# Layer 1 attention: a head's two score blocks merged into one ahead of the softmax, and the turned block masked twice out of PSUM

## What is computed

```python
nb = s // WINDOW                                  # 8 blocks of 128 tokens
kk = jnp.concatenate([prev(kb), kb], axis=2)      # keys of the block before and of the own block
vv = jnp.concatenate([prev(vb), vb], axis=2)
scores = jnp.einsum('bnqhgd,bnkhd->bnhgqk', qb, kk) * (SWA_HEAD_DIM ** -0.5)
valid = ((rel >= 0) & (rel < WINDOW))[None] & ...
scores = jnp.where(valid[None, :, None, None], scores, -jnp.inf)
m = jnp.maximum(jnp.max(scores, axis=-1), sink)
p = jnp.exp(scores - m[..., None])
denom = jnp.sum(p, axis=-1) + jnp.exp(sink - m)
o = jnp.einsum('bnhgqk,bnkhd->bnhgqd', p, vv) / denom[..., None]
```

## Time and profile before

| what | value |
|---|---|
| median of 3 runs | 2116.43 us (2115.18 to 2119.19) |
| the profiled execution | span 2115.3 us, 1.1 under the median and 0.1 over the fastest run |
| PE busy | 2045.7 us, 97% |
| DVE busy | 1604.8 us, 76% |
| ACT busy | 1361.3 us, 64% |
| POOL busy | 277.7 us, 13% |
| the attention of layer 1 | about 1224 to 1461 us of the span |

### The profile page before, as it was taken

How to read it: one execution, slowest core, us unless ns; L and a number is a source line. 1 busy time by engine, 2 the same in 40 slices (tenths; PEclk the granted TensorE clock), 3 DMA queues, 4 the chain that set the end, 5 groups by cost and what they waited for, 6 DMA issues and landing times. The chain is left out here.

```text
span 2115.3 us, 30221 instructions
## 1 busy us (share of the span) xinstructions
PE 2045.7 (97%) x10536; PEld 1661.4 (79%) x10536; DVE 1604.8 (76%) x2000; ACT 1361.3 (64%) x1794; POOL 277.7 (13%) x334
## 2 busy tenths in 40 slices
PE   8999998998999999999999989999899999999998
PEld 6888876787788888888877856777688888888885
DVE  4551246777888888888886267887898888888886
ACT  5333426653788887878772266675577778888774
POOL 2000000001111121111203320110111111122210
PEclk9999999999999999999999999999999999999999
DMA  4112222215999999999983020011699999999996
GB/s 139 40 60 90 78 72 78 81 65 205 343 381 390 389 389 385 380 378 380 385 317 132 1 90 11 21 61 61 231 383 380 381 384 384 387 388 385 384 363 254
DMA packets 123491, 513.28 MB, mean 243 GB/s; under 512 B 27373, under 2 KB 28490, under 8 KB 89610
## 3 DMA queue, kind: packets, MB, share of 16 engines
q1 hardware_dynamic: 103674, 474.11, 59.7%
q0 software_dynamic: 18576, 33.86, 4.2%
q10 hardware_dynamic: 1152, 4.19, 0.5%
HBM read 495.05 MB, written 50.86 MB: 258 GB/s over the span
## 5 line engine op out<-in xcount | busy, mean ns | idle before, releaser
L542 DVE TENSOR_TENSOR exp_w_lo<-ring_raw,first_w_hi 128x2048 fp32r<-128x2048 f32 x192 | 438.9, 2288 | 33.2 <-ACT first_w_hi L469 33.1
L542 DVE TENSOR_TENSOR exp_w_lo<-ring_raw,exp_w_hi 128x2048 fp32r<-128x2048 f32 x192 | 438.8, 2287 | 27.8 <-ACT exp_w_hi L469 27.8
L469 ACT ACTIVATE exp_w_hi<-ring_raw 128x2048 fp32r<-128x2048 f32 x192 | 367.7, 1918 | 62.1 <-PE exp_up_out L394 27.9
L469 ACT ACTIVATE first_w_hi<-ring_raw 128x2048 fp32r<-128x2048 f32 x188 | 360.7, 1919 | 62.2 <-PE exp_up_out L394 23.6
L339 POOL DMA_INDIRECT y_rows<-exp_y,base_rows_y x63 | 79.8, 1266 | 936.1 <-ACT exp_y L489 936.1
L394 PE MATMUL exp_gate_out<-exp_w_lo,exp_x_hi 128*128 128x512 f32 x512 | 201.1, 393 | 0.0
L394 PE MATMUL exp_y_out<-exp_w_lo,exp_hid_hi 128*128 128x512 f32 x512 | 200.4, 391 | 0.0
L394 PE MATMUL exp_up_out<-exp_w_lo,exp_x_hi 128*128 128x512 f32 x512 | 199.3, 389 | 0.0
L546 DVE TENSOR_TENSOR exp_x_lo<-exp_x_turned,exp_x_hi 128x1024 fp32r<-128x1024 f32 x62 | 75.9, 1224 | 51.4 <-ACT exp_x_hi L473 51.4
L394 PE MATMUL exp_gate_out<-first_w_hi,exp_x_hi 128*128 128x512 f32 x272 | 109.7, 403 | 3.1 <-issue 2.0
L350 POOL DMA_INDIRECT first_x_rows<-u_rows,base_rows_u x64 | 104.9, 1639 | 58.6 <-issue 52.2
(11 more groups left out here) (529 smaller groups left out, 4671.8 us busy)
## 6 DMA issues: line engine op xcount, KB each, us to landing
ring_raw<-in_expert_w_gate_dram SPq DMA_DIRECT2D x128, 1024.0 KB, 11.1
ring_raw<-in_expert_w_up_dram SPq DMA_DIRECT2D x128, 1024.0 KB, 11.6
ring_raw<-in_expert_w_down_dram SPq DMA_DIRECT2D x128, 1024.0 KB, 11.4
l0w_raw<-in_ab_w_in_dram SPq DMA_DIRECT2D x48, 256.0 KB, 2.8
finish_y<-y_rows SPq DMA_DIRECT2D x8, 1024.0 KB, 12.4
ring_raw<-in_swa_w_qkv_dram SPq DMA_DIRECT2D x5, 1024.0 KB, 10.1
ring_raw<-y_rows SPq DMA_DIRECT2D x10, 512.0 KB, 4.9
base_h<-in_x_dram ACTq DMA_DIRECT2D x8, 512.0 KB, 7.0
```

Of the source, the lines that this page charges most:

```text
L469: nc.scalar.activation(split[split_slot(unit)][0][:], raw[raw_slot(unit)][:], ACT.Copy).then_inc(hi_ready, 1)
L542: nc.vector.tensor_tensor(lo[:], raw[raw_slot(unit)][:], hi[:].bitcast(F32), ALU.subtract).then_inc(lo_ready[split_slot(unit)], 1)
```

## The change

The two blocks of a head are merged before the softmax: one 128x128 block holds the own block's score where k <= q and that of the block before where k > q. For G >= 4 `copy_own` (new, ACT) copies the own block's 512 columns out of PSUM into `masked`, and `mask` overwrites the places k > q with the block before by `copy_predicated` under `tri_strict` (DVE, out of PSUM); for G < 4 `mask` adds the large negative number there. The scale moves into the exponential and into the negative top. Maximum, exponentials, sums and scalings then run over 128 columns a head, and `turn` has four transposes, into one bank of `turned`, alternately the first and the second. Instead of ACT's copies, DVE's `band_probs` (new) multiplies the turned block out of PSUM by each of two complementary masks (`band`) into the two halves of `prob_t`: the block before first, then the own one. `weigh` is as it was. On DVE the order becomes `band_probs(G)`, `denominators(G+1)`, `mask(G+2)`, `out_low(G)`; on ACT `copy_own(G+2)` and `norm_even(G+1)` come ahead of `out_high(G)`. The table `units` becomes two units at each of its eight places.

```diff
@@ -833,7 +833,7 @@
...
-        ("swa_add", [P, 2, P], F32),
+        ("band", [P, 2, P], F32),
...
@@ -868,7 +868,7 @@
...
-                        ("causal_add", 0.0), ("last_row", 0.0), ("swa_add", 0.0), ("lr_up", 0.0)):
+                        ("causal_add", 0.0), ("last_row", 0.0), ("band", 1.0), ("lr_up", 0.0)):
...
@@ -882,9 +882,9 @@
...
-    for slot, (pattern, step), op in ((0, up, ALU.is_gt), (1, down, ALU.is_ge)):
-        part = c["swa_add"][:, slot]
-        nc.gpsimd.affine_select(out=part, in_=part, pattern=pattern, compare_op=op, fill=NEG,
+    for slot, (pattern, step), op in ((0, down, ALU.is_gt), (1, up, ALU.is_ge)):
+        part = c["band"][:, slot]
+        nc.gpsimd.affine_select(out=part, in_=part, pattern=pattern, compare_op=op, fill=0.0,
...
@@ -2291,11 +2291,13 @@
...
+        by_head = lambda x: x.rearrange("p (h n) -> p h n", h=PER)
...
-        masked = [work[n][:] for n in (3, 4, 5)]
+        masked = [work[n][:, 0:BANK] for n in (3, 4, 5)]
+        turned_at = lambda G: turned[:, PER * (G % 2):PER * (G % 2 + 1)]
...
@@ -2602,20 +2604,15 @@
...
-                n = G // GROUPS
...
-                p_of = heads4(masked[G % 3])
-                for b in range(0 if n else 1, 2):
-                    if b == 0 and G > GROUPS:
-                        pe.wait_ge(s["early_copied"], G - GROUPS)
-                    if b == 1 and G > 0:
-                        pe.wait_ge(s["prob_copied"], G)
-                    for i in range(PER):
-                        last = nc.tensor.transpose(turned[:, PER * b + i], p_of[:, i, b], c["ident"][:])
-                    last.then_inc(s["prob_turned" if b else "early_turned"], 1)
+                if G > 1:
+                    pe.wait_ge(s["own_made"], G - 1)
+                for i in range(PER):
+                    last = nc.tensor.transpose(turned_at(G)[:, i], by_head(masked[G % 3])[:, i], c["ident"][:])
+                last.then_inc(s["prob_turned"], 1)
...
@@ -2627,9 +2624,9 @@
...
-                        pe.wait_ge(s["early_copied"], G - GROUPS + 1)
+                        pe.wait_ge(s["prev_made"], G - GROUPS + 1)
...
-                        pe.wait_ge(s["prob_copied"], G + 1)
+                        pe.wait_ge(s["own_made"], G + 1)
...
@@ -2706,7 +2703,7 @@
...
-            units = {(0, 0): (0, 3), (0, 1): (3, 4), (1, 0): (4, 7), (1, 1): (7, 8), (2, 0): (8, 9), (2, 1): (9, 10), (3, 0): (10, 14), (3, 1): (14, 16)}
+            units = {(0, 0): (0, 2), (0, 1): (2, 4), (1, 0): (4, 6), (1, 1): (6, 8), (2, 0): (8, 10), (2, 1): (10, 12), (3, 0): (12, 14), (3, 1): (14, 16)}
...
@@ -2822,31 +2819,25 @@
                 a.activation(w_hi[:, k], w_raw[:, k], ACT.Copy).then_inc(s["w_hi_made"], 1)
 
             def exponents(G):
-                j, first = G % 3, 0 if G >= GROUPS else P
+                j = G % 3
                 act.wait_ge(s["tops_made"], G + 1)
                 for i in range(PER):
-                    span = slice(i * 2 * P + first, (i + 1) * 2 * P)
-                    a.activation(masked[j][:, span], masked[j][:, span], ACT.Exp, bias=neg_top[j][:, i:i + 1], accum_out=total[j][:, i:i + 1])
+                    own = by_head(masked[j])[:, i]
+                    a.activation(own, own, ACT.Exp, bias=neg_top[j][:, i:i + 1], scale=HEAD_DIM ** -0.5, accum_out=total[j][:, i:i + 1])
                 a.activation(sink_part[j][:], sink_part[j][:], ACT.Exp).then_inc(s["prob_made"], 1)
 
             def norm_even(G):
-                j, first = G % 3, 0 if G >= GROUPS else P
+                j = G % 3
                 act.wait_ge(s["inv_made"], G + 1)
                 for i in range(2):
-                    span = slice(i * 2 * P + first, (i + 1) * 2 * P)
-                    last = a.activation(masked[j][:, span], masked[j][:, span], ACT.Copy, scale=inv[j][:, i:i + 1])
+                    own = by_head(masked[j])[:, i]
+                    last = a.activation(own, own, ACT.Copy, scale=inv[j][:, i:i + 1])
                 last.then_inc(s["even_normed"], 1)
 
-            def copy_turned(G):
-                if G >= 1:
-                    act.wait_ge(s["out_ready"], G)
-                for b in range(0 if G >= GROUPS else 1, 2):
-                    if b == 0:
-                        act.wait_ge(s["early_turned"], G - GROUPS + 1)
-                    else:
-                        act.wait_ge(s["prob_turned"], G + 1)
-                    part = slice(PER * b, PER * (b + 1))
-                    a.activation(prob_t.rearrange("p (k q) -> p k q", q=P)[:, part], turned[:, part], ACT.Copy).then_inc(s["prob_copied" if b else "early_copied"], 1)
+            def copy_own(G):
+                act.wait_ge(s["scored"], G + 1)
+                act.wait_ge(s["prob_turned"], G - 2)
+                a.activation(by_head(masked[G % 3]), heads4(scores)[:, :, 1], ACT.Copy).then_inc(s["own_copied"], 1)
 
             def out_high(G):
                 n, g = G // GROUPS, G % GROUPS
...
@@ -2904,11 +2895,13 @@
             exponents(1)
             for G in range(LAST):
                 g, w = G % GROUPS, G // GROUPS - 2
+                if 1 < G < LAST - 2:
+                    copy_own(G + 2)
                 if w >= 0 and g < 2:
                     router_cols(w, g)
-                copy_turned(G)
+                if G < LAST - 1:
+                    norm_even(G + 1)
                 if G == 0:
-                    norm_even(1)
                     exponents(2)
                 if G in W_O_HIGH_AT:
                     w_o_high(W_O_HIGH_AT[G][0])
...
@@ -2917,8 +2910,6 @@
...
-                if 0 < G < LAST - 1:
-                    norm_even(G + 1)
...
@@ -2997,33 +2988,43 @@
                 last.then_inc(s["keys_made"], 1)
 
             def mask(G):
-                g, j, first = G % GROUPS, G % 3, 0 if G >= GROUPS else 1
-                by_head = lambda x: x.rearrange("p (h b k) -> p h b k", h=PER, b=2)[:, :, first:].rearrange("p h b k -> p h (b k)")
-                dve.wait_ge(s["scored"], G + 1)
-                if G >= 3:
-                    dve.wait_ge(s["prob_turned"], G - 2)
-                v.scalar_tensor_tensor(by_head(masked[j]), by_head(scores), HEAD_DIM ** -0.5, bc(c["swa_add"][:, first:].rearrange("p b k -> p (b k)"), 1, PER), ALU.mult, ALU.add)\
-                    .then_inc(s["masked_made"], 1)
+                g, j = G % GROUPS, G % 3
+                if G < GROUPS:
+                    dve.wait_ge(s["scored"], G + 1)
+                    if G >= 3:
+                        dve.wait_ge(s["prob_turned"], G - 2)
+                    v.scalar_tensor_tensor(by_head(masked[j]), bc(c["tri_strict"][:].bitcast(F32), 1, PER), NEG, heads4(scores)[:, :, 1], ALU.mult, ALU.add)\
+                        .then_inc(s["masked_made"], 1)
+                else:
+                    dve.wait_ge(s["own_copied"], G - GROUPS + 1)
+                    v.copy_predicated(by_head(masked[j]), bc(c["tri_strict"][:].bitcast(U32), 1, PER), heads4(scores)[:, :, 0]).then_inc(s["masked_made"], 1)
                 dve.drain()
                 v.tensor_reduce(top[j][:], by_head(masked[j]), AX.X, ALU.max)
                 dve.drain()
                 ordered = lambda x: x[:, PER * g:PER * (g + 1)].rearrange("p (i o) -> p o i", o=2)
                 pairs = lambda x: x[:].rearrange("p (o i) -> p o i", o=2)
-                v.scalar_tensor_tensor(pairs(neg_top[j]), pairs(top[j]), -1.0, ordered(neg_sinks), ALU.mult, ALU.min)
+                v.scalar_tensor_tensor(pairs(neg_top[j]), pairs(top[j]), -HEAD_DIM ** -0.5, ordered(neg_sinks), ALU.mult, ALU.min)
                 dve.drain()
                 v.tensor_tensor(pairs(sink_part[j]), ordered(c["sinks"]), pairs(neg_top[j]), ALU.add).then_inc(s["tops_made"], 1)
 
             def denominators(G):
-                j, first = G % 3, 0 if G >= GROUPS else P
+                j = G % 3
                 dve.wait_ge(s["prob_made"], G + 1)
                 v.tensor_tensor(inv[j][:], total[j][:], sink_part[j][:], ALU.add)
                 dve.drain()
                 v.reciprocal(inv[j][:], inv[j][:]).then_inc(s["inv_made"], 1)
                 dve.drain()
                 for i in range(2, PER):
-                    span = slice(i * 2 * P + first, (i + 1) * 2 * P)
-                    last = v.tensor_scalar(masked[j][:, span], masked[j][:, span], inv[j][:, i:i + 1], None, ALU.mult)
+                    own = by_head(masked[j])[:, i]
+                    last = v.tensor_scalar(own, own, inv[j][:, i:i + 1], None, ALU.mult)
                 last.then_inc(s["odd_normed"], 1)
+
+            def band_probs(G):
+                dve.wait_ge(s["prob_turned"], G + 1)
+                if G >= 1:
+                    dve.wait_ge(s["out_ready"], G)
+                for b in range(0 if G >= GROUPS else 1, 2):
+                    v.tensor_tensor(by_head(prob_t[:, b * BANK:(b + 1) * BANK]), turned_at(G), bc(c["band"][:, b], 1, PER), ALU.mult).then_inc(s["own_made" if b else "prev_made"], 1)
 
             def out_low(G):
```

(11 more changed lines are left out.)

## The result

| | before | after |
|---|---|---|
| median of ten runs (us) | 2118.85 (2115.18 to 2120.12) | 2124.1 (2120.3 to 2128.93) |
| ratio after / before | | 1.0026, 95% interval 1.0017 to 1.0035 |
| profiled execution: span | 2115.3 | 2127.2 |
| TensorE's mean granted clock in it | 0.990 | 0.985 |

The change makes the kernel 0.26% slower, 3.6 to 7.4 us by the interval and 5.3 by the medians: inside the range, but just past the 0.2% that I had as "no change", on the slower side. Of the 6.5 us between my 2117.6 and 2124.1, 2.4 are that the kernel before came out at 2118.85 here and not at the 2116.43 I started from.

A forecast was written before the change was run, and what follows sets the result against it. The prediction took PE to bound the kernel, VectorE nearly as full and deciding most steady groups after the change. Its terms summed to +1.2 us, 2116.5 by the profiled span, forecast as 2117.6 us, no tellable change, range 2109 to 2125.

The forecast's parts named there:

- up to G = 6: Start, "up to G = 5" in the forecast: VectorE decides before and after, with the low output weights; 0 (-1 to +1).
- G = 6 to 10: Groups without experts yet: PE decides and gains four times 0.42 us from the removed transposes; -1.7 us.
- G = 10 to 14: Groups with the first expert choices: PE decides three, VectorE one; 27.9 against 28.53 us, -0.6.
- three tiles, G = 14 to 26: VectorE decides three of a tile's four groups, moved units lengthen the fourth; +1.0, +1.3, +1.3, so +3.6 us.
- G = 26 to 30: Tile without score and queries in its last group: about 28.8 against 28.58 us, +0.2.
- turn(30) and the tail: Wait for `norm_even` and slower steps behind it go, -1.5 us; two more products in VectorE's tail, +1.2.
- Rival 3: The predicated copy costs as much as the old mask did: +8.7 us, 2126; chance 0.10.
- The steady tile: G = 18 to 22: 30.17 us against 28.91, +1.3 a tile, with PE waiting some 3 us.
- two lanes: In each steady group, VectorE's load and PE's own interval; the longer sets the group's length, 30.17 us a tile.
- the ring: Found after the forecast: a tile is VectorE's queue to the last scores' copy, then PE's work to the next tile's turn.
- Rival 1: PE keeps the pace everywhere, so its removed work counts: 2103 us, halfway 2110; chance 0.16.
- Rival 2: PE's waits pull its clock down, in one group in each of five tiles: +7.5 us, 2125; chance 0.14.

The follow-up runs named there:

- run 1: The changed kernel with the old table of output projection units; 2124.42 us, 1.0029 to the kernel before.
- run 3: The changed kernel with all four scalings of a group on ScalarE; 2112.58 us, 0.9977 to the kernel before.
- run 9: The changed kernel with another table of units (1, 2, 2, 3, 1, 2, 2, 3), one unit instead of two before turn(22); 2118.84 us, 1.0003.
- run 5: The changed kernel with the edits of run 2, run 3 and run 4 together; 2105.66 us, 0.9944 to the kernel before.
- run 10: The kernel of run 5 with another table of units (2, 3, 3, 2, 1, 1, 2, 2); 2103.97 us, 0.9938 to the kernel before.
- run 2: The changed kernel with some low parts of the output weights made one group later on VectorE; 2121.91 us, 1.0025 to the kernel before.
- run 4: The changed kernel with ScalarE copying the whole turned block and VectorE making one product instead of two; 2113.33 us, 0.9978 to the kernel before.
- run 7: The kernel before with ScalarE's scalings of G+1 ahead of the exponentials of G+2; 2114.6 us, 0.9986.

## Why the prediction was right and where it was wrong

From turn(0) to the experts, by its own steps (predicted, then measured in the profiled pair, us):

| step | predicted | measured |
|---|---|---|
| up to G = 6 | 0 | +1.7 (G = 0 to 4 -1.8, G = 4 to 6 +3.5) |
| G = 6 to 10 | -1.7 | -1.4 |
| G = 10 to 14 | -0.6 | -0.2 |
| three tiles, G = 14 to 26 | +3.6 | +4.2 (1.3, 1.5, 1.4) |
| G = 26 to 30 | +0.2 | -0.2 |
| turn(30) and the tail | -0.3 | +1.7 |
| sum | +1.2 | +5.9 |

The sum is off by 4.7 us in all, of which 1.7 lie ahead of G = 6 and 2.0 behind turn(30).

**Prices.** All held: copy 0.72 us (0.71), products 0.686 (0.68), maximum 0.686 (0.69), four transposes 0.35 to 0.42 us. ScalarE at nothing held too: from 1250 to 1450 PE has no wait for it. Rival 3 is out.

**The steady tile** held in sum: 30.43 for 30.17, PE waiting 3.18 us ("some 3"), in the two places named. Its mechanism did not. I had each group as the longer of two lanes, 6.82, 7.31, 7.66 and 8.38 us. The turns came at 6.07, 7.23, 7.60 and 9.53. PE does not wait out VectorE's lateness group by group: the lateness is carried on and paid at once. The two sums agree on this kernel and part on its edits: run 1 gave 30.33 where the lanes give 28.8, run 3 28.81 where they give 29.2, run 9 29.73 where they give no change, and the ring accounts for all three. That the sum was right is thus in part luck: the 1.38 us that I charged to the moved units did not hang on the table. Rival 1, PE at its own pace, is out for the changed kernel, and is what runs 5 and 10 show once VectorE and ScalarE are relieved.

**The step that failed** is the first, "up to G = 5 ... 0". I saw that VectorE's low parts of the weights lie there, but not that the copy of the turned block moved **behind** them when it moved from ScalarE to VectorE. VectorE's queue ahead of the products of G = 4, and what PE then waits for:

```profile
1267.69 2.36 DVE L2962 TENSOR_TENSOR l_w_lo<-l1r_w_raw,l_w_hi 128x1024 fp32r<-128x1024 f32 x2
1270.08 1.29 DVE L3027 TENSOR_TENSOR l_work<-l_turned,base_band 128x512 f32<-128x512 f32 x2
1270.91 1.38 PE L2631 MATMUL l_wide<-l_work,l_vals 128*64 128x256 f32 x8 [2.74 <-DVE l_work L3027]
```

From G = 4 to 6 the changed kernel takes 3.5 us more, with this wait and 8 us at a clock of 0.57 behind it (window above); 1.8 were won before. Run 2 took 0.95 of the 3.5 back. Runs 3, 4 and 5, which take work out of VectorE's queue in every group, took back 2.7, 2.4 and 2.5 in the same stretch. In run 5 the low clock, 0.57 again, lasted some 4 us (1267.07 to 1271.07, and 1.00 behind it).

**The tail.** The wait at turn(30) is gone and the slow clock behind it too; run 7 shows that the order on ScalarE does it. From turn(30) to `weigh(30)` it is 1.92 us for 3.18, with four transposes less and a unit more. I had this right, and missed what came behind:

```profile
1460.90 0.60 PE L2614 MATMUL l_turned<-base_ident,l_work 128*128 128x128 f32 x4
...
1462.82 1.08 PE L2631 MATMUL l_wide<-l_work,l_vals 128*64 128x256 f32 x8
...
1477.51 3.46 PE L2683 MATMUL l_turned<-base_router,ring_raw 128*128 128x36 f32 x16
```

The two products stand in VectorE's tail for 1.29 us as counted. The clock is lower, too: from 1470 to 1500 it is 0.83 throughout, where the three windows of before that answer to it, 1460 to 1490, have 1.00, 1.00 and 0.83; sixteen router products take PE 3.46 us there for 1.87. From `weigh(30)` to the experts the four executions with this tail took 43.4, 44.3, 44.9 and 45.4 us, three with the tail of before 42.4, 42.4 and 43.2: +1.8 on average, for the 1.2 that I had put down for the products. In the profiled pair it is 3.0. No run took the products or the clock of the tail out by itself, so how the rest divides stays open.

**Rival 2**, the clock, is right in kind and wrong in place. Its sign to look for, dips between 1280 and 1450, did not come: that window has 1.00 throughout, though PE waits there in every tile. The dips are at G = 4, behind the longest wait that the change adds, and in the tail. What they cost is not separated from the waits around them: run 2 did not settle it. I also misread a row in my argument against this rival: the window 1254 to 1256 ends inside the wait of 1.29 us. The two us behind the wait, 1256 to 1258, do have 1.00.

So the sum was right in its largest term and short by two others: a queue that I had not read, and a tail whose cost is in part open. The upper end of my range, 2125, came from the price of rival 2, which did not happen in the tiles; that 2124.1 lies just under it is luck.

## What to carry to other kernels

When a step moves to another engine, read what stands ahead of it in that engine's queue in every stage, the rare ones too, not only its price in the steady stage. Where two engines wait for each other once in several groups, follow the ring to the last wait on each side: work inside it counts at full price, and work outside is free until it opens a further wait (run 1), so a rebalance can be placed rather than balanced. An edit that frees one engine and fills another wants the next job moved as well: the same two scalings were worth -11.5 us after the change and +18 before it.

## What the hardware showed that I had not expected

VectorE pays the same for 512 elements from PSUM and from SBUF: products 686 ns out of PSUM in after, 688 ns out of SBUF in run 4. One ScalarE copy of the same 512 elements takes 575 to 595 ns, less than either. The length of a wait alone does not tell whether PE's clock falls. After the 2.74 us wait it fell to 0.57 for 8 us; waits of 0.5 and 0.7 us in the tiles, and one of 1.25 us at 1379 in run 9, left it at 1.00. But in the kernel before the wait of 1.42 us at turn(30) was followed by 0.50 (1450.80 to 1453.98), and a longer one, at turn(5), by 1.00 (1270.51 to 1277.67):

```profile
1270.51 1.09 PE L2617 MATMUL l_turned<-base_ident,l_work 128*128 128x128 f32 x8 [1.96 <-ACT l_work L2837]
```

No run took apart what else it depends on.
